# Hybrid decoder layer with 32 experts on one core: the final norm's weight spread in expert 5, and expert 30's down product between the gate-up halves of expert 31

## The reference

```python
def expert_block(args):
    xb, eid = args
    gu = xb @ w_gate_up[eid] + b_gate_up[eid]
    gate = jnp.minimum(gu[:, :D_FF], SWIGLU_LIMIT)
    up = jnp.clip(gu[:, D_FF:], -SWIGLU_LIMIT, SWIGLU_LIMIT)
    glu = gate * jax.nn.sigmoid(gate * SWIGLU_ALPHA)
    return ((up + 1.0) * glu) @ w_down[eid] + b_down[eid]
```

## Time and profile before

| what | value |
|---|---|
| median of 3 runs | 1030.42 us (1030.27 to 1030.55) |
| profiled execution | 1030.68 us, its span 1028.9 us |
| TensorE busy | 1003.6 us, 98% of the span |
| VectorE, ScalarE busy | 264.3 us, 149.4 us |
| moved | 423.97 MB, mean 412 GB/s |

### The profile page before, as it was taken

The page is one execution under the profiler, slowest core; times in us unless marked ns, Lnnn a source line. Parts: engine busy times, 40 slices in busy tenths (PEclk is TensorE's granted clock), DMA queues, the critical chain, the costliest instruction groups (busy, mean ns, idle before and its releaser), DMA issues.

```text
span 1028.9 us, 12532 instructions
## 1 busy us (share of the span) xinstructions
PE 1003.6 (98%) x5012; PEld 414.6 (40%) x5012; DVE 264.3 (26%) x658; ACT 149.4 (15%) x299; POOL 9.7 (1%) x27
## 2 busy tenths in 40 slices
PE   9999999999999999999999999999999999999997
PEld 7799833333333333333333333333333333333333
DVE  2866232122122122212222122221221212122122
ACT  1311211111111111111111111111111111111112
POOL 1010000000000000000000000000000000000000
PEclk9999999999999999999999999999999999999999
DMA  9975899999999999999999999999999999999996
GB/s 380 398 323 204 343 400 425 427 427 435 428 429 430 434 431 428 433 432 431 434 431 428 433 432 431 436 429 428 433 432 431 434 431 428 428 426 426 426 422 247
DMA packets 24716, 423.97 MB, mean 412 GB/s; under 512 B 3048, under 2 KB 3696, under 8 KB 6384
## 3 DMA queue, kind: packets, MB, share of 16 engines
q1 hardware_dynamic: 23328, 420.78, 96.3%
q10 hardware_dynamic: 1360, 2.79, 0.7%
HBM read 422.51 MB, written 1.05 MB: 412 GB/s over the span
## 4 chain that ended last, share of the span: by engine, by line
PE 81%; DMA 18%; issue 1%; ACT 0%; DVE 0%; SPq 0%; POOL 0%; another core or an unknown queue 0%; ACTq 0%; PEldq 0%; DVEq 0%; POOLq 0%
PE bank L1675 33%; PE bank L1695 19%; DMA ring<-in_w_expert 18%; PE bank L1363 5%; PE y L1739 5%; PE bank L1561 5%; PE bank L1714 3%; PE y L1524 2%; PE bank L1617 1%; PE bank L1413 1%; PE bank L1355 1%; PE bank L1524 1%; PE bank L1720 1%; PE bank L1797 1%; PE y L1781 0%
## 5 line engine op out<-in xcount | busy, mean ns | idle before, releaser
L1675 PE MATMUL bank<-ring,x_t 128*64 128x512 f32 x1984 | 447.1, 597 | 0.0
L1695 PE MATMUL bank<-ring,act 128*64 128x512 f32 x992 | 230.6, 596 | 11.3 <-DMA ring<-in_w_expert 11.3
L1675 PEld LDWEIGHTS bank<-ring,x_t 128*64 128x64 f32 x1984 | 133.9, 136 | 261.9 <-issue 258.4
L1219 DVE TENSOR_TENSOR gu_b<-bank,bias_t 128x512 f32<-128x512 f32 x64 | 44.2, 691 | 326.9 <-PE bank L1714 326.8
L1695 PEld LDWEIGHTS bank<-ring,act 128*64 128x64 f32 x992 | 68.4, 137 | 142.3 <-issue 140.8
L759 ACT COPY gu_sb<-bank 128x512 f32<-128x512 f32 x64 | 37.5, 586 | 222.7 <-PE bank L1675 222.7
L1172 DVE TENSOR_TENSOR x_t<-bank,cols 128x512 f32<-128x512 f32 x30 | 20.7, 691 | 165.0 <-PE bank L1617 165.0
L1739 PE MATMUL y<-z,p_t 64*128 64x512 f32 x248 | 61.6, 615 | 0.0
L1561 PE MATMUL bank<-x_sb,p_row 128*64 128x512 f32 x256 | 60.6, 593 | 0.0
L1158 DVE TENSOR_SCALAR p_row<-slot,rank,rstd 128x64 f32<-128x64 f32 x62 | 16.6, 312 | 164.5 <-PE bank L1720 164.5
L763 ACT ACTIVATE act<-gu_b 128x256 f32<-128x256 f32 x62 | 25.8, 417 | 192.2 <-DVE gu_b L1225 192.2
(11 more groups left out here) (247 smaller groups left out, 509.1 us busy)
## 6 DMA issues: line engine op xcount, KB each, us to landing
ring<-in_w_expert SPq DMA_DIRECT2D x66, 4096.0 KB, 33.7
ring<-in_w_expert SPq DMA_DIRECT2D x48, 2048.0 KB, 17.3
ring<-in_w_expert SPq DMA_DIRECT2D x18, 1024.0 KB, 10.7
ring<-in_w_in SPq DMA_DIRECT2D x4, 2048.0 KB, 27.7
ring<-in_w_out SPq DMA_DIRECT2D x2, 2048.0 KB, 28.0
ring<-in_w_in SPq DMA_DIRECT2D x2, 1024.0 KB, 13.3
ring<-in_w_expert SPq DMA_DIRECT2D x4, 512.0 KB, 4.4
ring<-in_w_down_last SPq DMA_DIRECT2D x4, 512.0 KB, 28.5
```

The source lines that it names most:

```text
L1219: dve.tensor_tensor(gu_b[:, :, :, :], bank[2][:, :].rearrange("p (f a s) -> p a f s", a=2, f=4), bias_t[:, :, 4 * h:4 * h + 4, ds(e, 1)] . ...
L1675: ins = mm(bank[h][a * SLOTS:(a + 1) * SLOTS, :], x_t_of(it)[:, k, :], w[:, kk, a, :], start=k == 0, stop=k == KT - 1)
L1695: ins = mm(bank[0][a * SLOTS:(a + 1) * SLOTS, :], act_of(it)[:, k, :], w[:, kk, a, :], start=k == 0, stop=k == KT - 1)
```

## The change

Two things are moved. g is loaded at the end of expert 4 (`COUNT_AT`) and spread within expert 5 (`SPREAD_AT`) into memory of tensors that are no longer used then (`bdn`, `gates_t`, `before`, `chosen` and others, laid side by side for it). And in the last two experts the load order becomes a0 to a3, b0, b1, a4, a5, b2 to b5, with TensorE's work in that order. Expert 30's down product goes to PSUM bank 3 and its copy to `z_prev`; its scatter is cut by token tile and stands around the second half of b3, ahead of b's last turn.

```diff
-    order += [(it, j) for it in (E - 2, E - 1) for j in range(4)]
-    return order + [(it, j) for it in (E - 2, E - 1) for j in range(4, ITEM_CHUNKS)]
+    order += [(E - 2, j) for j in range(4)] + [(E - 1, j) for j in range(2)]
+    return order + [(E - 2, j) for j in range(4, ITEM_CHUNKS)] + [(E - 1, j) for j in range(2, ITEM_CHUNKS)]
...
-        return place_in_order(it, j) + 1
+        return place_in_order(it, j) + (0 if it == E - 1 and j >= 2 else 1)
...
-        g_bc = at("g_bc", [P, D], slot_at(SPARE[0]) + 8192)
+        z_prev = at("z_prev", [P, HALF], slot_at(SPARE[0]) + 8192)
...
                 keep_p_t(b)
-                for h in range(2):
-                    keep_gate_up(b, h)
-                    sigmoid(b, h)
-                keep_z(a)
+                keep_gate_up(b, 0)
+                sigmoid(b, 0)
+                keep_z(a, bank[3])
+                keep_gate_up(b, 1)
+                sigmoid(b, 1)
...
-            act_e.wait_ge(s_pref, 1)
-            act_e.dma_start(g8[:, :], norm_final_g.rearrange("(k p) -> k p", p=P)).then_inc(s_gfin, 16)
+                if it == COUNT_AT:
+                    act_e.wait_ge(s_pref, 1)
+                    act_e.dma_start(g8[:, :], norm_final_g.rearrange("(k p) -> k p", p=P)).then_inc(s_gfin, 16)
...
-                for h in range(2):
-                    activate_half(it, it, h)
+                activate_half(it, it, 0)
+                if isinstance(it, int) and it == SPREAD_AT:
+                    for h in range(2):
+                        dve.wait_ge(s_gb, h + 1)
+                        dve.tensor_copy(g_bc[:, h * HALF:(h + 1) * HALF], bank[3][:, :]).then_inc(s_gbk, 1)
+                activate_half(it, it, 1)
...
                 gate_up(it, 3, range(4))
+                if known == SPREAD_AT:
+                    pe.wait_ge(s_gfin, 16)
+                    pe.wait_ge(s_table, 1)
+                    broadcast_g(0)
                 pe.wait_ge(s_av, number(it) * 2 + 1)
                 down(it, 4, range(0, 2))
+                if known == SPREAD_AT:
+                    pe.wait_ge(s_gbk, 1)
+                    broadcast_g(1)
                 turn(it, 1)
...
                 gate_up(b, 1, range(4))
-                gate_up(b, 2, range(0, 2))
-                turn(b, 0)
-                gate_up(b, 2, range(2, 4))
-                gate_up(b, 3, range(4))
+                pe.wait_ge(s_ptk, b + 1)
                 pe.wait_ge(s_av, 2 * b)
                 down(a, 4, range(0, 2))
-                turn(b, 1)
+                turn(b, 0)
                 down(a, 4, range(2, 4))
                 down(a, 5, range(4))
+                gate_up(b, 2, range(4))
+                gate_up(b, 3, range(0, 2))
+                scatter(a, [0])
+                gate_up(b, 3, range(2, 4))
+                scatter(a, [1])
+                turn(b, 1)
 
                 pe.wait_ge(s_av, 2 * b + 1)
-                down_half(0, range(0, 2))
-                scatter(a)
-                down_half(0, range(2, 4))
+                down_half(0, range(0, 4))
```

More of the change, by code:

```diff
@@ L92 @@
 PAIRED = range(LOOP_FROM, LOOP_TO)
-COUNT_AT, FILL_AT, SUMS_AT, ROWS_AT = 4, 5, 4, (4, 5)
+COUNT_AT, FILL_AT, SUMS_AT, ROWS_AT, SPREAD_AT = 4, 5, 4, (4, 5), 5
 assert LOOP_FROM % 2 == 0 and (LOOP_TO - LOOP_FROM) % 2 == 0 and RING == 2 * ITEM_CHUNKS
-assert max(COUNT_AT, FILL_AT, SUMS_AT, *ROWS_AT) < LOOP_FROM
+assert COUNT_AT < FILL_AT <= SPREAD_AT and SUMS_AT < SPREAD_AT and max(SPREAD_AT, *ROWS_AT) < LOOP_FROM
 class InLoop:
@@ L203, in build @@
         act, gu_b = row((("act", [P, F // P, SLOTS], f32), ("gu_b", [P, 2, 4, SLOTS], f32)), 16384, 20480)
-        (p_t, bdn, gates_t, bias_t, ident, ones, before, slot1, gates, rank1, chosen, table,
+        (p_t, bdn, gates_t, before, chosen, lmax, four, hot, bias_t, ident, ones, slot1, gates, rank1, table,
          cols, ss, ss3, rest, root, var, lnv, rstd, tmp2, eps_c, one_c, n_items, cnt, more, block_c, boff_c, exp_c, place, extra1,
-         hot, n_f, lmax, four, ngt, ssh, minus_half) = row((
+         n_f, ngt, ssh, minus_half) = row((
              ("p_t", [P, T], f32), ("bdn", [P, HALF], f32), ("gates_t", [P, TT, P], f32),
-             ("bias_t", [P, 2, F // P, E], f32), ("ident", [P, P], f32),
-             ("ones", [P, P], f32), ("before", [P, P], f32), ("slot1", [P, P], f32), ("gates", [P, TT, E], f32),
-             ("rank1", [P, TT, E], f32), ("chosen", [P, TT, E], f32), ("table", [1, 2 * TABLE], i32),
+             ("before", [P, P], f32), ("chosen", [P, TT, E], f32), ("lmax", [P, TT, 8], f32), ("four", [P, TT, 8], f32),
+             ("hot", [E, BLOCKS - 1, EXTRA], f32), ("bias_t", [P, 2, F // P, E], f32), ("ident", [P, P], f32),
+             ("ones", [P, P], f32), ("slot1", [P, P], f32), ("gates", [P, TT, E], f32),
+             ("rank1", [P, TT, E], f32), ("table", [1, 2 * TABLE], i32),
              ("cols", [P, NCOLS], f32), ("ss", [P, TT], f32),
@@ L216, in build @@
              ("exp_c", [E, 1], f32), ("place", [E, BLOCKS - 1], f32), ("extra1", [E, EXTRA], f32),
[L217 to L220, removed]
+             ("n_f", [1, BLOCKS - 1], f32), ("ngt", [P, TT], f32), ("ssh", [P, 2, TT], f32), ("minus_half", [P, 1], f32)), 20480, KEPT)
+        g_at = 20480 + 1024
+        before_at = g_at + 2048 + 1024
+        bias_at = before_at + 512 + 256 + 2 * 64 + 192
+        table_at = bias_at + 2048 + 3 * 512 + 2 * 256
+        assert g_at + 4 * D <= bias_at
+        g_bc = at("g_bc", [P, D], g_at)
         g8 = at("g8", [KT, P], before_at)
@@ L280, in x_t_of, with z_of @@
             return x_t_last if isinstance(it, int) and it == E - 1 else x_t
+        def z_of(it):
+            return z_prev if isinstance(it, int) and it == E - 2 else z
         def p_t_of(it):
@@ L763, in sigmoid, with keep_z @@
                 act_e.activation(act_of(it)[:, 4 * h:4 * h + 4, :], gu_b[:, 0, :, :], ACT.Sigmoid, scale=ALPHA).then_inc(s_sig, 1)
-            def keep_z(it):
+            def keep_z(it, src=bank[0]):
                 act_e.wait_ge(s_dn, it + 1)
-                act_e.copy(z[:, :], bank[0][:, :]).then_inc(s_z, 1)
+                act_e.copy(z_of(it)[:, :], src[:, :]).then_inc(s_z, 1)
             def evacuate(it, following):
@@ L1256, in activate_last_two @@
                 place_next(a)
-                for h in range(2):
-                    dve.wait_ge(s_gb, h + 1)
-                    dve.tensor_copy(g_bc[:, h * HALF:(h + 1) * HALF], bank[3][:, :]).then_inc(s_gbk, 1)
                 activate_half(a, a, 0)
@@ L1694, in down @@
                     for a in range(2):
-                        ins = mm(bank[0][a * SLOTS:(a + 1) * SLOTS, :], act_of(it)[:, k, :], w[:, kk, a, :],
+                        dst = bank[3 if isinstance(it, int) and it == E - 2 else 0]
+                        ins = mm(dst[a * SLOTS:(a + 1) * SLOTS, :], act_of(it)[:, k, :], w[:, kk, a, :],
                                  start=k == 0, stop=k == KT - 1)
@@ L1727, in gather_next, with scatter @@
                 gather()
-            def scatter(it):
+            def scatter(it, ts=range(TT)):
                 pe.wait_ge(s_z, number(it) + 1)
@@ L1735, in scatter @@
                     pe.wait_ge(s_more, 1)
-                for t in range(TT):
+                for t in ts:
                     for nn in range(2):
                         r = slice(nn * SLOTS, (nn + 1) * SLOTS)
-                        mm(y_ps[t][nn][:, :], p_t_of(it)[r, t * P:(t + 1) * P], z[r, :],
+                        mm(y_ps[t][nn][:, :], p_t_of(it)[r, t * P:(t + 1) * P], z_of(it)[r, :],
                            start=first, stop=False, skip_group_check=True).then_inc(s_y, 1)
@@ L1768, in products @@
                     pe.wait_ge(s_hot, 1)
-                if known == FILL_AT:
-                    pe.wait_ge(s_table, 1)
+                if known == SPREAD_AT:
+                    pe.wait_ge(s_gbk, 2)
                 if following is not None:
@@ L1814, in products_last_two @@
                 gate_up(a, 1, range(4))
-                pe.wait_ge(s_ptk, a + 1)
-                pe.wait_ge(s_gfin, 16)
-                broadcast_g(0)
                 gate_up(a, 2, range(0, 2))
-                pe.wait_ge(s_gbk, 1)
-                broadcast_g(1)
                 turn(a, 0)
                 gate_up(a, 2, range(2, 4))
-                pe.wait_ge(s_gbk, 2)
                 gather_next(a)
```

## The result

The changed kernel took 1034.52 us (median of 7 runs, 1032.86 to 1035.38) against 1030.55 us (7 runs, 1029.97 to 1030.88): ratio 1.0033, 95% interval 1.0024 to 1.0043, so 2.5 to 4.4 us slower. The profiled execution took 1034.46 us, its span 1032.7.

The account below looks back on a forecast made before the run. The end was taken as a weight arrival plus the TensorE work behind it. Later arrival +1.5 and clock fall +1.8 gave +3.3 us on 1030.42, so 1033.7 us, own range 1032.5 to 1035.2; 1031.3 to 1035.2 holds the first two cases.

Parts of the forecast that it names:

- The case without a fall: TensorE's stop before b2 does not lower the clock: +1.5 us, 1031.9 us, within 0.2%; chance 0.27.
- Step 1: Expert 5: spreading g there adds 2.16 us of TensorE work, covered by the weight queue's 5.4 us lead; 0 at the end.
- Step 2: Load order of the last two experts: each place keeps its old landing time, b2 at 1003.6, b3 at 1008.6.
- Step 3: Before b2, loaded whole with one semaphore: TensorE is done at 1000.3 and idles some 3.4 us until 1003.7.
- Step 4: TensorE work behind b2's arrival: 18.10 us plus the activation stall, ending at 1022.3 against 1020.83, so +1.5 us.
- S: TensorE's stall for the activation, behind the turn and four ks of half down: 0.5 us, bounds 0 and 0.9.
- Step 5: The 3.4 us stop before b2 drops the clock to 1.2 GHz: 1.8 us lost, middle of 0.6 and 3.0.
- The clock as a case of its own: Later arrival plus a clock fall in the stop before b2 is the forecast, +3.3 us, chance 0.58; no fall, 0.27.
- A starved stream in expert 5: Rival: spreads plus a wait for g eat the 5.4 us request slack; at most some 3 us more, 1035 to 1036.
- b2 is not waited for: Rival at the last experts: places 188 and 189 land 1.3 us or more sooner for TensorE; -1.2 us, 1029.2.
- the slower case: Whole kernel slower by over 0.2%, from 1032.5 us on; chance 0.64.

Follow-up runs that it names:

- the three compared above: Kernel before, changed kernel's g move alone, and its new order alone: last landings 1018.7, 1017.9, 1020.4 us; the latter two took 1030.97 and 1033.03 us.

## Why the prediction was right, point by point

- **Forecast +3.3 us (1033.7), measured +3.97 (1034.52), in a later session +2.6.** The mechanism was the one named: a later arrival that counts, and a clock that falls in the stop ahead of it. The case without a fall, given 0.27, is what a third of the runs do. The prediction weighed the fall as yes or no for the kernel, not as a mix of its runs; how near the median comes to the forecast hangs in part on that mix.
- **Step 1, g spread in expert 5: 0.** Right. TensorE is 2.16 us later, the request 2.6, the landing isn't (0.4 of the 325.7 is this execution's shifted stream, which shows at 1019.0 for the last landing too).
- **Step 2, the landings keep their places.** Right: b2 at 1004.0 against 1003.6 for the same place before, the last at 1019.0 against 1018.7.
- **Step 3, b2 as a whole is the arrival that counts.** Right, and shown by cutting it. The stop was 2.99 us (3.4 forecast); most of the difference is a wait of 0.23 for the piece before and a last group of 8 records that takes 1.94 to its end where I took 1.77. The wait's place and releaser are those forecast; with b2 in halves it is the landing of b3's first half that counts.
- **Step 4, the order costs +1.5 us.** A size slightly off: 1.8 by three profiles. The half scatters take 1.06 us each, not half of 1.92, so two of them add 0.2. The stall for the activation was 0.43 where S was 0.5.
- **Step 5, a fall costs 1.8 us.** Measured 1.7 between profiles (13.7 less 12.0), 2.1 between the medians of runs with and without. My bounds of 0.6 and 3.0 came from the start's long stretch; here the low level lasted no longer than from 1004 to 1007.6. That the middle of two bounds so far apart came within 0.1 us was luck: no row of the kernel before had a fall in the middle of work.
- **The clock as a case of its own.** Both profiles of the changed kernel show 0.50 behind a stop of 2.99 us, and one profile each 1.00 behind stops of 0.56, 1.14 and 1.66 us; but 6 of 18 runs went without the loss, so at this stop it is a matter of odds. No profile has a stop between 1.8 and 2.99 us, so where the odds begin stays open. The Trainium skill (TensorE: Matmul & The Clock Gate, Why this matters for your kernels) warns of idle gaps between bursts; the two profiles agree with it, the six runs show that this gap doesn't always do it.
- **The rivals.** A starved stream in expert 5 is out (only g moved, ratio 0.9998). That b2 is not waited for is out, by the stop of 2.99 us. The 1034.5 lies in the range, and the slower case had the largest chance.

## What to carry to other kernels

Work that waits for loads ends with an arrival, and a semaphore for a whole chunk at the wrong place can cost 2.6 us as here, so when loads are reordered the cuts into pieces have to move with the places. Taking work off TensorE in a stretch where it waits gains nothing and can lose: here the stop was 1.14 us with the spreading in expert 30 and 2.99 without it, and with the longer one the clock fell in most runs. Two edits are to be timed apart as well as together: here one costs 0, the other 2.0 us, and both 2.6 to 4.0.

## What the runs showed of the hardware that was not expected

- Ten matmuls on dead data gave back what the clock is worth: 13.7 to 12.0 us behind the last landing in the profiles.
- The fall is not tied to the stop alone: the same program with the same 3 us stop fell in 11 of 18 runs by their mean clock, and not in 6. Both profiles of it show the fall. What decides, the runs don't say.
- The weight landings differ by up to 2.5 us between executions (last landing 1017.9 to 1020.4 in nine profiles), and in the three compared above the difference already stands near 198 us. Runs of the kernel before spread over as much, 1029.62 to 1032.79 in the last session; that the one comes from the other fits, but isn't shown, since only profiles have landings.
